# Five of the input chunks as seven block products each, in one phase, with the results kept in DRAM

## The reference, cut to what matters

```python
u = rms_norm(x, norm_in_g)
h = u @ w_in                       # 1024 x 4096: pool_x, pool_z, m_x, m_z, 1024 columns each
pool_x, pool_z, m_x, m_z = split(h, 4)
pooled = [window_mean_minus_self(pool_x[g], w) for g, w in enumerate((2, 4, 8, 16))]  # 4 groups of 256
pool   = einsum(pooled, pool_w) * pool_scale * silu(pool_z)
c      = silu(conv5(m_x) + conv_b)              # five taps along the positions
q, k   = headwise(c, w_q), headwise(c, w_k)     # 4 x 4 blocks on the diagonal
v      = headwise(m_x, w_v)
gates  = concat(q, k, v) @ w_gates + b_gates    # input and forget gates, two directions, 4 heads
m      = mlstm(q, k, v, gates) * silu(m_z)      # chunks of 128 positions, forwards and backwards
x      = x + concat(pool, m) @ w_out
```

## Time and profile before

| | |
|---|---|
| time of three runs, us | 1169.72 median, 1169.14 to 1171.07 |
| span of the profiled execution, us | 1168.5 (the page gives no other time for it) |
| PE busy | 1158.7, 99% |
| DVE busy | 678.5, 58% |
| POOL busy | 455.9, 39% |
| ACT busy | 359.2, 31% |
| moved by DMA | 93.56 MB, 80 GB/s in the mean |

### The profile page before, as it was taken

How to read it: one execution, slowest core, us unless ns; L and a number is a source line. 1 busy time by engine, 2 the same in 40 slices (tenths; PEclk the granted TensorE clock), 3 DMA queues, 4 the chain that set the end, 5 groups by cost and what they waited for, 6 DMA issues and landing times.

```text
span 1168.5 us, 17252 instructions
## 1 busy us (share of the span) xinstructions
PE 1158.7 (99%) x6599; PEld 946.1 (81%) x6599; DVE 678.5 (58%) x1249; ACT 359.2 (31%) x720; POOL 455.9 (39%) x437
## 2 busy tenths in 40 slices
PE   9999999999999999999999999999999999999997
PEld 6888888888888868888878888878988887777786
DVE  5645557334368502157777883894699434556668
ACT  6312121100012212445665631242111134553322
POOL 2424222223333223354657656304223323455534
PEclk9999999999999999999999999999999999999999
DMA  7321121343312112300113242123121130133113
GB/s 241 109 81 45 36 81 36 123 152 114 109 36 72 64 64 90 101 23 23 50 34 112 88 171 73 72 100 95 40 88 36 37 100 1 38 122 124 39 38 141
DMA packets 75075, 93.56 MB, mean 80 GB/s; under 512 B 13938, under 2 KB 54090, under 8 KB 74483
## 3 DMA queue, kind: packets, MB, share of 16 engines
q1 hardware_dynamic: 67270, 88.73, 22.7%
q10 hardware_dynamic: 7724, 3.74, 1.2%
HBM read 75.11 MB, written 18.92 MB: 80 GB/s over the span
## 4 chain that ended last, share of the span: by engine, by line
PE 93%; DVE 4%; DMA 1%; ACT 1%; issue 1%; POOL 0%; ACTq 0%; DVEq 0%; POOLq 0%
PE bank L918 22%; PE bank L920 22%; PE bank L919 22%; PE bank L1219 4%; PE bank L1194 4%; PE wide L1210 2%; PE wide L1412 2%; PE bank L1158 1%; PE bank L1147 1%; PE bank L1135 1%; PE wide L920 1%; PE wide L919 1%; PE wide L918 1%; PE bank L1387 1%; DVE h L1910 1%; PE wide L1387 1%
## 5 line engine op out<-in xcount | busy, mean ns | idle before, releaser
L687 POOL CAST whi<-wraw 128x2048 fp32r<-128x2048 f32 x31 | 58.8, 1898 | 454.1 <-PE bank L920 404.1
L918 PE MATMUL bank<-u_hi,wlo 128*128 128x512 f32 x488 | 190.4, 390 | 0.0
L920 PE MATMUL bank<-u_hi,whi 128*128 128x512 f32 x488 | 189.9, 389 | 0.0
L919 PE MATMUL bank<-u_lo,whi 128*128 128x512 f32 x488 | 189.9, 389 | 0.0
L689 POOL TENSOR_TENSOR wlo<-wraw,whi 128x2048 fp32r<-128x2048 f32 x32 | 153.1, 4784 | 3.0 <-ACT whi L2488 0.5
L918 PE MATMUL bank<-x_hi,wlo 128*128 128x512 f32 x312 | 123.5, 396 | 0.0
L920 PE MATMUL bank<-x_hi,whi 128*128 128x512 f32 x312 | 121.6, 390 | 0.0
L919 PE MATMUL bank<-x_lo,whi 128*128 128x512 f32 x312 | 121.5, 389 | 0.0
L918 PEld LDWEIGHTS bank<-u_hi,wlo 128*128 128x128 f32 x488 | 91.6, 188 | 19.9 <-POOL wlo L689 0.8
L920 PEld LDWEIGHTS bank<-u_hi,whi 128*128 128x128 f32 x488 | 91.6, 188 | 19.0
L919 PEld LDWEIGHTS bank<-u_lo,whi 128*128 128x128 f32 x488 | 91.6, 188 | 18.9
(11 more groups left out here) (391 smaller groups left out, 2440.9 us busy)
## 6 DMA issues: line engine op xcount, KB each, us to landing
wraw<-in_w_in SPq DMA_DIRECT2D x26, 1024.0 KB, 5.5
wraw<-in_w_out SPq DMA_DIRECT2D x12, 1024.0 KB, 5.1
xr<-in_x SPq DMA_DIRECT2D x8, 512.0 KB, 7.3
hst<-in_x SPq DMA_DIRECT2D x4, 1024.0 KB, 5.0
hpool<-hst SPq DMA_DIRECT2D x4, 1024.0 KB, 4.1
smz<-mzs SPq DMA_DIRECT2D x16, 256.0 KB, 2.0
h<-hpool SPq DMA_DIRECT2D x4, 1024.0 KB, 7.5
resid<-h SPq DMA_DIRECT2D x8, 512.0 KB, 2.6
```

The source lines that it names most:

```text
L687: g_.tensor_copy(whi[w % 2][:, :, :], wraw[:, :, :]).then_inc(s["w_hi"], 1)
L918: pe.matmul(ps, al, bh, start=(k == 0), stop=False)
L919: pe.matmul(ps, ah, bl, start=False, stop=False)
L920: return pe.matmul(ps, ah, bh, start=False, stop=(k == nk - 1))
```

## The change

The eight pool chunks and eight m chunks of w_in come in another order, and five of them are computed in another way.

- Chunks 2 to 6 of the new plan (columns 8, 9, 6, 5 and 4 of w_in in units of 256: two chunks of m_x and three of pool_z) are each formed from seven block products. The chunk is seen as a 2 by 2 matrix of blocks: two halves of 128 of its columns by two halves of 512 positions, each a sum over two halves of the input features. Seven products of combined blocks replace the eight. A product takes four steps over 512 input features, three matmuls each, so 12 matmuls, and 84 for a chunk (`seven`).
- The combined blocks of u (Tf, with parts Thi and Tlo, four of them) are made once, by POOL (`first_half`) and DVE, parts by ACT and DVE. The combined blocks of the weights (xsum, and in place in wraw) are made by POOL for each chunk; their hi parts by ACT (`cast_block`), their lo parts by POOL and DVE (`low_block`).
- DVE adds the products up (`add_up`) into two tiles of sz; SyncE stores them, the m_x ones raw to umraw, the pool_z ones, after silu, to szpool, and loads them again when they are used. The two m_x chunks are loaded into um behind the pool products.
- The first m_z chunk (column 12) is now chunk 1. The plan then has the three other pool_x chunks and the fourth pool_z chunk; the mixes follow one chunk behind their windows, and the last mix stands right behind the groups of that pool_z chunk (`mix(3)`). Behind the pool products come two chunks of m_x and three of m_z; between the pool products and the gate sums there are three chunks (they were five).
- Semaphores of later stages are used again for the new counts (`early`, `used`).

```diff
-        plan += [("w_in", g, "f"), ("w_in", 4 + g, "f")]
+    plan = [("w_in", c, "f") for c in (0, 12, 8, 9, 6, 5, 4, 1, 2, 3, 7)]
     plan += [("w_out_pool", c, "o") for c in (0, 2, 1, 3)]
-    plan += [("w_in", 8 + h, "f") for h in range(4)]
-    plan += [("w_in", 12 + h, "f") for h in range(4)]
+    plan += [("w_in", c, "f") for c in (10, 11, 13, 14, 15)]
...
+SEVEN = range(2, 7)
...
-    W_POOL, W_OP, W_MX, W_MZ, W_OM, W_2 = 0, 8, 12, 16, 20, 24
+    W_POOL, W_SZ3, W_OP, W_MX, W_MZ, W_OM, W_2 = (0, 7, 8, 9), 10, 11, 13, 16, 20, 24
...
+            sp_.wait_ge(s["t_gemm"], first[W_MX + 2])
+            for i in range(2):
+                sp_.dma_start(um[:, 2 * i:2 * i + 2, :], um_d[:, 2 * i:2 * i + 2, :]).then_inc(s[f"l_um{i}"], 16)
...
+            g_.wait_ge(s["v_ulo"], 8)
+            first_half(T3, 0)
             g_.wait_ge(s["v_xn"], NT)
-            for w in range(1, W_MX + 2):
+            split(1)
+            first_half(T4, 1)
...
+            for c in range(N7):
+                g_.wait_ge(s["l_w0"], 16 * (c + 2))
+                g_.wait_ge(s["l_wraw"], 16 * (S0 + c + 1))
+                step(g_.tensor_tensor(xs, raw(1, 0), raw(1, 1), ALU.add))
+                step(g_.tensor_tensor(raw(1, 0), raw(0, 0), raw(1, 0), ALU.subtract))
+                low_block(c, 2, xs)
+                g_.wait_ge(s["g_blk"], 4 * c + 1)
+                step(g_.tensor_tensor(xs, xs, raw(0, 0), ALU.subtract))
+                low_block(c, 3, xs)
+                g_.wait_ge(s["g_blk"], 4 * c + 2)
+                g_.tensor_tensor(xs, raw(0, 1), xs, ALU.subtract).then_inc(s["g_m0"], 1)
+                g_.wait_ge(s["g_m0"], c + 1)
+                low_block(c, 4, xs)
+                low_block(c, 5, raw(1, 0))
+                g_.wait_ge(s["g_blk"], 4 * c + 4)
+            for w in range(W_POOL[1], W_MX + 3):
                 split(w)
...
+            group(W_POOL[0], 3, u_hi, u_lo, "a_px", 4)
...
+            for i in range(4):
+                group(1, i, u_hi, u_lo, "a_mz", i + 1)
...
+                for i, moving in enumerate(factors):
+                    ps = ring_7(*(("a_part", c + 1), ("v_sum", b0 + 1), ("v_sum", b0 + 6), ("v_sum", b0 + 2),
+                                  ("v_sum", b0 + 4), ("v_sum", b0 + 5), ("v_sum", b0 + 7))[i])
+                    if i < 2:
+                        pe.wait_ge(s["v_blk"], 2 * c + i + 1)
+                    elif i < 6:
+                        pe.wait_ge(s["g_blk"], 4 * c + i - 1)
+                    else:
+                        pe.wait_ge(s["w_lo"], S0 + c + 1)
+                    if c == 0 and i in LATE_T:
+                        pe.wait_ge(s["v_Tlo"], LATE_T[i])
+                    wh, wl = slot(whi, b0 + i), slot(wlo, b0 + i)
+                    for k in range(4):
+                        mm = three(ps[:, :], ((wh[:, k, :], wl[:, k, :]), (moving[0][:, k, :], moving[1][:, k, :])),
+                                   k, 4)
+                    mm.then_inc(s["t_prod"], 1)
+
+            LATE_T = {2: 1, 3: 2, 5: 3, 6: 4}
+            for c in range(N7):
+                seven(c)
...
+            for i in range(4):
+                group(W_POOL[1], i, u_hi, u_lo, "a_px", 4 + i + 1)
+                if i == 1:
+                    mix(0)
+            for g in (2, 3):
+                for i in range(4):
+                    group(W_POOL[g], i, u_hi, u_lo, "a_px", 4 * g + i + 1)
+                mix(g - 1)
+            for i in range(4):
+                group(W_SZ3, i, u_hi, u_lo, "a_sz", 6 + i + 1)
+            mix(3)
...
+            for h in (2, 3):
+                for i in range(4):
+                    group(W_MX + h, i, u_hi, u_lo, "a_um", 4 * (h - 2) + i + 1)
             for i in range(4):
-                group(W_MX, i, u_hi, u_lo, "a_um", i + 1)
-
-
-            for n in range(3):
-                for i in range(4):
-                    group(W_MX + n + 1, i, u_hi, u_lo, "a_um", 4 * n + 4 + i + 1)
-            for i in range(4):
-                group(W_MZ, i, u_hi, u_lo, "a_mz", i + 1)
+                group(W_MZ + 1, i, u_hi, u_lo, "a_mz", 4 + i + 1)
             pe.wait_ge(s["v_ga"], 6)
             pe.wait_ge(s["g_init"], 6)
             pe.wait_ge(s["a_c"], KT)
...
+            for g in (2, 3):
+                window(g, 0)
+                mixed(g - 1)
+                window(g, 1)
+                low_mix(g)
+            mixed(3)
...
-                ve.wait_ge(s["a_um"], 4 * h + 2 * m + 2)
+                if h < 2:
+                    ve.wait_ge(s[f"l_um{h}"], 16)
+                else:
+                    ve.wait_ge(s["a_um"], 4 * (h - 2) + 2 * m + 2)
...
                 if g == 3:
-                    ac.wait_ge(s["t_mix"], 16)
-                for i in range(4):
-                    n = 4 * g + i
-                    ac.wait_ge(s["v_yr"], n + 1)
-                    ac.activation(yp_hi[:, 2 * g + i // 2, (i % 2) * HALF:(i % 2 + 1) * HALF], yr[:, n % 2, :],
-                                  ACT.Copy).then_inc(s["a_yhi"], 1)
+                    ac.wait_ge(s["v_yr"], 12)
+                    for i in range(4):
+                        m, nh = i // 2, i % 2
+                        ps = filled(ac, "t_gemm", first[W_SZ3] + i + 1, "a_sz", 6 + i + 1)
+                        ac.activation(sz[:, m, nh * HALF:(nh + 1) * HALF], ps[:, :], ACT.Silu).then_inc(s["a_sz"], 1)
+                high_px(g, 1)
```

More of the change, by code:

```diff
@@ new lines, in load_sz @@
+            def load_sz(g):
+                sp_.wait_ge(s["v_yr"], 4 * g)
+                sp_.wait_ge(s["o_st0"], 16 * (N7 - 1))
+                sp_.wait_ge(s["o_st1"], 16 * (N7 - 1))
+                sp_.dma_start(sz[:, :, :], sz_d[:, 2 - g, :, :]).then_inc(s["l_sz"], 16)
+            for f in range(2):
+                halves(0, f)
+            for n in range(2):
+                store_mz(n, yr[:, n % 2, :])
+            halves(1, 0)
+            for n in range(2, 4):
+                store_mz(n, yr[:, n % 2, :])
@@ new lines, in _ @@
+            halves(1, 1)
+            for c in range(N7 - 1):
+                for f in range(2):
+                    if c + 2 < N7:
+                        halves(c + 2, f)
+                    elif f:
+                        sp_.wait_ge(s["g_blk"], 4 * N7)
+                        wt(W_POOL[1])
+                    store_7(c, f)
+            wt(W_POOL[2])
+            sp_.wait_ge(s["v_px"], 3)
+            mix_weights(1)
+            wt(W_POOL[3])
+            load_sz(1)
+            sp_.wait_ge(s["v_px"], 8)
@@ L513, in rows_h @@
+            mix_weights(2)
+            wt(W_SZ3)
+            load_sz(2)
+            wt(W_OP)
+            sp_.wait_ge(s["v_px"], 13)
+            mix_weights(3)
+            wt(W_OP + 1)
+            sp_.wait_ge(s["v_px"], 20)
             def rows_h(q):
@@ L793, in units @@
                         heads_blocks(h + 1)
-            split(W_MX + 5)
-            split(W_MX + 6)
-            split(W_MX + 7)
-            split(W_OM)
+            for w in range(W_MX + 4, W_OM + 1):
+                split(w)
             heads_blocks(0)
@@ L1095, in _ @@
                     mm.then_inc(s["t_gate"], 1)
-            for i in range(4):
-                group(W_MZ + 2, i, u_hi, u_lo, "a_mz", 8 + i + 1)
-                if i == 0:
+                if i == 1:
                     pe.wait_ge(s["v_gs"], 4)
@@ L2257, in _, with cast_block @@
                 high_u(n)
-            pooled(0, 0)
-            pooled(0, 1)
-            for g in range(4):
+            def cast_block(c, i):
+                b = 7 * c + i
+                if i < 2:
+                    ac.wait_ge(s["l_w0"], 16 * (c + 2))
+                elif i == 4:
+                    ac.wait_ge(s["g_m0"], c + 1)
+                elif i == 6:
+                    ac.wait_ge(s["l_wraw"], 16 * (S0 + c + 1))
+                else:
+                    ac.wait_ge(s["g_part"], 7 + 3 * c + {2: 1, 3: 3, 5: 2}[i])
+                name, value = slot_free(b)
+                ac.wait_ge(s[name], value)
+                src = (raw(0, 0), raw(0, 1), xs, xs, xs, raw(1, 0), raw(1, 1))[i]
+                ac.activation(slot(whi, b), src, ACT.Copy).then_inc(s["a_wc"], 1)
@@ L2273, in _ @@
-                for i in range(4):
-                    m, nh = i // 2, i % 2
-                    ps = filled(ac, "t_gemm", first[2 * g + 1] + i + 1, "a_sz", 4 * g + i + 1)
-                    ac.activation(sz[:, m, nh * HALF:(nh + 1) * HALF], ps[:, :], ACT.Silu).then_inc(s["a_sz"], 1)
-                    if i < 2:
-                        ac.wait_ge(s["v_px"], 5 * g + i + 1)
-                        ac.activation(pxhi[:, i, :], px[:, i, PAD:PAD + S], ACT.Copy).then_inc(s["a_mixhi"], 1)
-                if g == 3:
-                    ac.wait_ge(s["t_mix"], 16)
@@ new lines, in high_y @@
+            def high_y(n):
+                g, i = n // 4, n % 4
+                ac.wait_ge(s["v_yr"], n + 1)
+                if n == 12:
+                    ac.wait_ge(s["t_mix"], 16)
```

(35 more changed lines are left out.)

448 lines of the change are left out of this document (323 added, 125 removed).

## The result

The changed kernel takes 1183.16 us (median, 1178.61 to 1184.61) against 1169.77 for the kernel before: ratio 1.0107, 95% interval 1.0088 to 1.0127. It is slower, by 13.4 us or 1.1%; 1180.7 was forecast, in a range of 1169 to 1190.

A forecast was written before the change was run, and what follows sets the result against it. TensorE, busy 99% of the span, was taken to bound the kernel. -13.6 + 2.5 + 3.2 + 16.8 + 2.1 = +11.0 us on 1168.5 gave 1179.5, with the median 1.2 above: 1180.7; range 1169 to 1190.

The forecast's parts named there:

- Products: Five chunks on PE: 84 matmuls instead of 96 each, at 0.2267 us, take off 13.6 us.
- The sum at the start: POOL's new sum into Tf holds DVE's scaling of x tile 5, so PE waits 2.5 us; bounds 0 and 3.5.
- The product phase: Seven-product chunks: POOL, ACT, DVE and weight loads keep ahead of PE's 19.0 us per chunk; cost 0.
- The two tight places: Before the first product, 4 us to spare; the split behind the phase, 1.5 us; 1 to 4 us if missed.
- term 2: POOL's new first_half sum at the start, ahead of chunk 1's split, makes PE wait: +2.5 us.
- The last mix: Before mix(3), the px cast behind the fourth silu and DVE's low part after POOL's CAST make PE wait 3.2 us.
- The convolution: Gate sums wait for eight convolved slices, started late and held by POOL's splits, with three chunks as cover: +16.8 us.
- it would just fit without POOL: Without POOL's port holds, the convolution's last silu at +64.7 us would precede PE's arrival at +65.3.
- The clock: PE's granted clock falls after the long convolution wait, losing 2.1 us once; 0 taken after the shorter waits.
- terms 2 and 3: Waits of 2.5 us at the start and 3.2 before the last mix; clock loss taken 0, bound 2 each.
- term 4: The convolution's wait before the gate sums: +16.8 us, bounds 7.8 and 19.
- Columns: Behind the gate sums, the chain through gates and rows keeps its length; columns ready 2 us ahead of PE, cost 0.

The follow-up runs named there:

- e12: e11 with the weight chunk behind the block products loaded and split in two halves of 128 columns; 1158.40 us, ratio 0.9900.
- e1: Changed kernel with ACT's cast of the last pool group's second px half moved between the second and third gate silu; 1176.12 us, ratio 1.0057.
- e4: Changed kernel with POOL's split of chunk 19 held until DVE has finished the eighth convolved slice; 1177.65 us, ratio 1.0074.
- e5: Changed kernel with um loaded ahead of the wait for the last hpool stores and chunk 16 split ahead of the Amat products; 1178.01 us, ratio 1.0064.
- e6: Changed kernel with the edits of e4 and e5 together; 1171.80 us, ratio 1.0012.
- e3: Changed kernel with POOL's splits of chunks 17, 18 and 19 cut to 8 of 256 columns, so m_z lacks its own weights; 1165.52 us, ratio 0.9966.
- e2: Changed kernel with POOL's first sum into Tf behind the split of chunk 1 instead of ahead of it; 1186.87 us, ratio 1.0143.
- e9: e8 with DVE's two window means of the first pool group moved to the second and third chunk of products; 1169.74 us, ratio 1.0002.
- e11: e8 with the edits of e9 and e10 together; 1164.65 us, ratio 0.9962.
- e7: Changed kernel with POOL's first sum into Tf held until DVE has scaled all eight x tiles, still ahead of chunk 1's split; 1182.31 us, ratio 1.0101.
- e8: Changed kernel with the edits of e1, e7 and e6 together; 1168.18 us, ratio 0.9990.
- e10: e8 with ACT instead of POOL casting chunks 17 and 18, and um loaded in three pieces; 1163.49 us, ratio 0.9953.

## Why the prediction was right, and where it was off

**Products, -13.6.** Shown by e12: PE is busy for 1145.1 us where it was for 1158.7, 13.6 less, and with the waits gone the span agrees with the sum to 0.6 us.

**The sum at the start, forecast 2.5, measured 3.4.** The mechanism is right, the place one tile off in this execution: POOL's sum began 0.01 us ahead of the scaling that I had let pass first, and held it for the whole 4.6 us. Which of the two is first is a matter of 0.1 to 0.3 us. In the profiled executions of e1, e4, e5 and e6, whose start is the same code, the scaling went first, the next one was held, and the wait was 2.3 or 2.4 us; in e3 it was 3.4 again.

**The product phase, 0.** No wait in it in the changed kernel. The two tight places were tight: e2 met the first (1.2 us before the first product) and the second (2.0), e9 and e11 the second. A third, which I had not named, is DVE's window means among the sums of the first chunk of products: they cost 2.7 us in e7 and 2.8 in e8 and e10; e9, which moves them, is without that wait. What I hadn't seen either is that all were tied to term 2: PE's 3.4 us at the start are part of what kept them out of sight. Without that wait others of 2.7 (e7) to 6.4 us (e11) come in its place, so term 2 was never a gain to be had alone.

**The last mix, 3.2, measured 3.2.** e1 shows the cast's place to be the cause.

**The convolution, 16.8, measured 10.8 + 3.3 = 14.1.** The gate sums start 81.1 us behind the output products; 82.1 was forecast. The late start was right: the first scaling ended at +15.3, and DVE free at +14.5 with a scaling of 0.81 gives the same. The 1.0 us between 81.1 and 82.1 is for the most part the splits, which took 5.7 us each instead of 6.0. PE came at +70.3 instead of 65.3, held by the earlier wait of 3.3 and the clock, so a part of the sum stands under other names. e3, e4, e5 and e6 show both causes, the late start and the held taps, with 17.2 us for three splits. That it would just fit without POOL holds too: in e3 PE waits for nothing there. The Trainium skill, SBUF — State Buffer, section "SBUF: two separate sides", says that the pair of ports is locked for a whole instruction and the loser blocks fully. These traces agree: 5.52 us for a tap of 1.28 ahead of which a subtraction began that takes 4.6 alone.

**The clock, 2.1, measured 7.7.** This is the step that failed. I counted it for the long wait alone and took 0 for those of terms 2 and 3, "about as short as what the clock bore" by the last window of the span. The long wait cost 1.7 us of PE's work, near the 2.1 that I gave; the waits of 3.2 to 3.4 us cost 1.4 to 2.9 more each, 6.0 in all. I had a bound of 2 each for two of them, and should have put a value on it and not only a bound. The 2.1 itself was an inference: the weight loads of the earlier trace rows do go from 0.64 to 0.33 us apart, but the granted clock of those first microseconds reads 1.00 in the profile, so no row shows that it was the clock. That the sum came as near as it did, 11.0 forecast and 14.2 measured, is in part luck: 5.6 us too little for the clock stand against 2.7 too much in term 4.

**Columns, 0, measured 0.7.** I had them 2 us ahead.

## What to carry to other kernels

Fewer matmuls are worth their time only while the slower stage beside them still fits: here five chunks of cover became three, and the stage that it covered had no pause left into which POOL's SBUF work could fall. Before moving a DVE or POOL instruction, look for what the other has in SBUF at that time, and give the casts to ACT. And take the waits away from the last one backwards: a wait in front may only hide a later one, as e2, e7, e9 and e11 show.

## What was not expected of the hardware

The price of a wait of about 3 us is not fixed. The wait before the last mix is 3.2 us in the changed kernel and in e2. In the first the mean granted clock is 0.76 from 262 to 276; in e2, with the same wait, it stays up:

```profile
264.00:280.00 16.00, 12.84 (x57) 10.31 (x56) 5.15 (x7) 3.33 (x5) 7.35 (x2) 1.00 0.47 160
```

In e4, e5 and e6 the clock took 1.6 to 1.7 us there. The waits of 2.3 to 2.4 us near 25 cost 1.7 in e4, e5 and e6 and nothing in e1. What decides it in one execution stays open. The runs of the changed kernel spread over 6.0 us, those of e12, which has no wait over 1.0 us, over 0.7. The clock alone does not order them: the fastest of the changed kernel's runs, 1178.61, has a mean granted clock of 0.990, two slower ones 0.992. A split of chunk 19 that comes late, as in e7, would shorten a run; no trace of these runs shows it.

A POOL instruction keeps DVE out also when it starts 0.01 us ahead of it, and a form of 64 columns still costs: in e3 POOL's subtraction of 128x64, 0.3 us alone, took 1.3 us at 388.7, since it waited for a tap in its turn.
